# How the first two row blocks are picked out of the tokens in a Trainium2 mixture-of-experts kernel

## What is computed

```python
def moe_ffn(h, router_w, router_bias, w_gate, w_up, w_down):
    scores = jax.nn.sigmoid((t @ router_w).astype(jnp.float32))
    ...
    _, eidx = lax.top_k(jnp.where(emask, sel, -jnp.inf), TOP_K)
    ...
    hg = jnp.einsum('td,edf->tef', t, w_gate)
    hu = jnp.einsum('td,edf->tef', t, w_up)
    act = jax.nn.silu(hg) * hu * comb[:, :, None].astype(t.dtype)
    return jnp.einsum('tef,efd->td', act, w_down).reshape(B, L, D)
```

## Time and profile before

| | |
|---|---|
| runs, median | 1278.73 us |
| the profiled execution | 1281.8 us |
| its span on the core | 1280.1 us |
| PE busy | 1009.5 us (79%) |
| DVE, ACT, POOL busy | 416.9, 229.7, 192.8 us |
| mean granted TensorE clock | 0.907 of 2.4 GHz |
| DMA | 344.59 MB, mean 269 GB/s |

### The profile page before, as it was taken

One profiled execution on the slowest core, in us unless ns is written; L12 is line 12 of the kernel. 1 busy time (PEld: TensorE's weight loads), 2 busy tenths in 40 slices (PEclk: granted clock), 3 DMA queues, 4 the chain that ended last, 5 costly groups with the idle time before them and its releaser, 6 DMA issues.

```text
span 1280.1 us, 24187 instructions
## 1 busy us (share of the span) xinstructions
PE 1009.5 (79%) x9506; PEld 572.9 (45%) x9506; DVE 416.9 (33%) x1139; ACT 229.7 (18%) x459; POOL 192.8 (15%) x382
## 2 busy tenths in 40 slices
PE   0899999789699777796389998988979997775930
PEld 0444447554555444453245554445465553342510
DVE  0220015864612221122553234553542221111207
ACT  0401002431412111111221111110322121110202
POOL 1200000200122221222210000001022221211231
PEclk9999999899689998899689998999959998987975
DMA  9985332967479999999994211444631969999973
GB/s 317 383 277 197 131 139 91 352 246 307 173 278 389 393 402 411 393 396 369 393 378 145 92 66 48 182 197 148 251 160 42 378 236 401 395 398 413 396 274 131
DMA packets 79819, 344.59 MB, mean 269 GB/s; under 512 B 9158, under 2 KB 9609, under 8 KB 67468
## 3 DMA queue, kind: packets, MB, share of 16 engines
q1 hardware_dynamic: 57108, 289.30, 58.4%
q0 software_dynamic: 14608, 43.35, 9.7%
q10 hardware_dynamic: 8040, 11.01, 2.5%
HBM read 320.01 MB, written 23.63 MB: 268 GB/s over the span
## 4 chain that ended last, share of the span: by engine, by line
PE 60%; DMA 20%; DVE 11%; SPq 3%; ACT 3%; issue 2%; POOL 0%; POOLq 0%; DVEq 0%; ACTq 0%; PEldq 0%
PE bank L856 15%; DMA ring<-in_moe_w_up_dram 15%; PE bank L646 11%; PE bank L921 10%; PE bank L772 6%; PE bank L863 6%; DMA ring<-in_ada_w_dram 3%; SPq L1351 3%; PE bank L833 2%; DMA ring<-in_moe_w_down_dram 1%; PE bank L599 1%; PE bank L995 1%; PE bank L1019 1%; ACT arena L1204 1%; DVE arena L1320 1%
## 5 line engine op out<-in xcount | busy, mean ns | idle before, releaser
L856 PE MATMUL bank<-ring,arena 128*32 128x256 f32 x3072 | 193.5, 409 | 50.6 <-DMA ring<-in_moe_w_up_dram 50.6
L856 PEld LDWEIGHTS bank<-ring,arena 128*32 128x32 f32 x3072 | 104.9, 118 | 132.6 <-issue 78.2
L646 PE MATMUL bank<-ring,hT 128*128 128x512 f32 x336 | 144.9, 593 | 1.0 <-ACT hT L1055 1.0
L1318 DVE TENSOR_TENSOR arena<-arena,bank 128x64 f32<-128x64 f32 x136 | 27.4, 202 | 317.0 <-ACT arena L1204 317.0
L921 PE MATMUL bank<-hT,ring 128*128 128x384 f32 x384 | 124.6, 487 | 1.0 <-ACT hT L1055 1.0
L863 PE MATMUL bank<-ring,arena 128*32 128x256 f32 x1536 | 92.8, 382 | 27.3 <-DVE arena L1320 25.4
L599 PE MATMUL bank<-ring,small 128*32 128x256 f32 x768 | 53.8, 443 | 58.7 <-DMA ring<-in_ada_w_dram 58.7
L646 PEld LDWEIGHTS bank<-ring,hT 128*128 128x128 f32 x336 | 63.7, 190 | 80.4 <-issue 79.2
L921 PEld LDWEIGHTS bank<-hT,ring 128*128 128x128 f32 x384 | 72.9, 190 | 52.3 <-ACT hT L1055 1.2
L856 PE MATMUL bank<-arena 128*32 128x256 f32 x1216 | 72.8, 393 | 13.9 <-DMA arena<-in_moe_w_up_dram 13.9
L533 POOL DMA_DIRECT2D arena<-slot_rows x140 | 70.8, 506 | 59.6 <-POOL arena L543 42.8
(11 more groups left out here) (325 smaller groups left out, 1112.6 us busy)
## 6 DMA issues: line engine op xcount, KB each, us to landing
ring<-in_ada_w_dram SPq DMA_DIRECT2D x24, 2048.0 KB, 19.6
ring<-in_moe_w_gate_dram SPq DMA_DIRECT2D x22, 2048.0 KB, 21.9
ring<-in_moe_w_up_dram SPq DMA_DIRECT2D x22, 2048.0 KB, 27.2
ring<-in_moe_w_down_dram SPq DMA_DIRECT2D x22, 2048.0 KB, 30.1
arena<-in_moe_w_gate_dram SPq DMA_DIRECT2D x10, 2048.0 KB, 35.1
arena<-in_moe_w_up_dram SPq DMA_DIRECT2D x10, 2048.0 KB, 40.6
arena<-in_moe_w_down_dram SPq DMA_DIRECT2D x10, 2048.0 KB, 43.9
ring<-in_ev_w_in_dram SPq DMA_DIRECT2D x7, 2048.0 KB, 15.6
```

Of the source, the lines that this page charges most:

```text
L646: last = pe.matmul(bank[3 * (c % 2) + t], hT[:, k, t * P:(t + 1) * P], slot8(n)[:, k, :], start=k == 0, stop=k == KT - 1)
L856: last = pe.matmul(bank[1][q * BLK:(q + 1) * BLK, 0:HALF], slot_inT[:, k, :], both[:, :, k, q * P:(q + 1) * P], start=k == 0, stop=k == KT ...
L1318: dve.tensor_tensor(act_rows[:, two, :], silu_g[:, two, :], up, ALU.mult).then_inc(S["gated"], 1)
```

## The change

It has six parts, in both layers.

1. The picking of block 0 with `h_tok` stationary (L833) goes. Both blocks are picked with 32 columns of `pick` stationary and 512 columns of `h_tok` moving, in the four column groups: 12 matmuls in all.
2. Block 0 now takes the way of the other blocks: ScalarE copies it (64 partitions x 512) to `slot_in`, PE transposes it, DVE copies it to `slot_inT`. ScalarE copies block 1 to `slot_in` after a wait for those transposes.
3. Four matmuls with `ident` stationary and 512 columns of `h_tok` moving go to `bank[3]`, which nothing reads, ahead of the wait for `pick`.
4. PE waits for `table_rdy` and reads the first two limits of its loops before it waits for `pick_rdy`, not after the picking.
5. PE's wait for `trips_rdy` moves to the end of the layer.
6. POOL's wait on its own copies counts one more, since ScalarE now signals twice.

```diff
@@ pool_moe @@
-                    pool.wait_ge(S["row_rdy"], pair * 2 + odd)
+                    pool.wait_ge(S["row_rdy"], pair * 2 + (odd + 1))
@@ pe_moe @@
             pe.wait_ge(htok_act, 6 * (l + 1))
+            for c in range(WARM):
+                pe.matmul(bank[3], ident, h_tok[:, c % NT, 0:512], start=True, stop=True)
+            rows_due = counter(pe, f"rows_due{l}", 1)
+            pe.wait_ge(table_rdy, l + 1)
+            begin, end, after = 0, pe.value_load(table[0:1, 1:2], ...), pe.value_load(table[0:1, 2:3], ...)
             pe.wait_ge(pick_rdy, l + 1)
-            for k in range(KT):
-                h, j = divmod(k, 4)
-                for t in range(NT):
-                    last = pe.matmul(bank[0][:, j * 2 * BLK + h * BLK:j * 2 * BLK + (h + 1) * BLK], h_tok[:, t, k * P:(k + 1) * P],
-                                     pick[:, t, 0:BLK], start=t == 0, stop=t == NT - 1)
-            last.then_inc(S["rowT_mm"], 1)
             for t in range(NT):
                 for q in range(4):
-                    c = (q % 2) * 512 + (q // 2) * HALF
-                    last = pe.matmul(bank[2][q * BLK:(q + 1) * BLK, 0:HALF], pick[:, t, BLK:2 * BLK], h_tok[:, t, c:c + HALF],
-                                     start=t == 0, stop=t == NT - 1)
+                    block, h = divmod(q, 2)
+                    last = pe.matmul(bank[2][q * BLK:(q + 1) * BLK, :], pick[:, t, block * BLK:(block + 1) * BLK],
+                                     h_tok[:, t, h * 512:(h + 1) * 512], start=t == 0, stop=t == NT - 1)
             last.then_inc(pick_mm, 1)
-            pe.wait_ge(table_rdy, l + 1)
-            pe.wait_ge(trips_rdy, l + 1)
...
-            rows_due = counter(pe, f"rows_due{l}", 1)
             pe.sem_inc(S["rowT_mm"], 1)
-            begin, end = 0, pe.value_load(table[0:1, 1:2], ...)
+            rows_to_channels()
             for e in range(NE):
                 n = first + 3 * e
-                after = pe.value_load(table[0:1, e + 2:e + 3], ...) if e + 1 < NE else None
+                if e:
+                    after = pe.value_load(table[0:1, e + 2:e + 3], ...) if e + 1 < NE else None
...
+            pe.wait_ge(trips_rdy, l + 1)
             stores = pe.value_load(trips[0:1, 1:2], ...)
@@ act_moe @@
             act.wait_ge(pick_mm, l + 1)
-            act.activation(slot_in[:, 0:HALF], bank[2][0:2 * BLK, 0:HALF], ACT.Copy)
-            act.activation(slot_in[:, HALF:2 * HALF], bank[2][2 * BLK:4 * BLK, 0:HALF], ACT.Copy).then_inc(S["row_rdy"], 1)
+            act.activation(slot_in, bank[2][0:2 * BLK, :], ACT.Copy).then_inc(S["row_rdy"], 1)
+            act.wait_ge(S["rowT_mm"], 2)
+            act.activation(slot_in, bank[2][2 * BLK:4 * BLK, :], ACT.Copy).then_inc(S["row_rdy"], 1)
```

More of the change, by code:

```diff
@@ L48 @@
 MOE_RING = 9
+WARM = 4
 CHUNK = 4096
@@ L828, in pe_moe @@
             pe.wait_ge(htok_act, 6 * (l + 1))
-            pe.wait_ge(pick_rdy, l + 1)
-            for k in range(KT):
-                h, j = divmod(k, 4)
-                for t in range(NT):
-                    last = pe.matmul(bank[0][:, j * 2 * BLK + h * BLK:j * 2 * BLK + (h + 1) * BLK], h_tok[:, t, k * P:(k + 1) * P],
-                                     pick[:, t, 0:BLK], start=t == 0, stop=t == NT - 1)
-            last.then_inc(S["rowT_mm"], 1)
+            for c in range(WARM):
+                pe.matmul(bank[3], ident, h_tok[:, c % NT, 0:512], start=True, stop=True)
+            rows_due = counter(pe, f"rows_due{l}", 1)
+            pe.wait_ge(table_rdy, l + 1)
+            begin, end, after = 0, pe.value_load(table[0:1, 1:2], min_val=1, max_val=MAX_BLOCKS), pe.value_load(table[0:1, 2:3], min_val=2, max_val=MAX_BLOCKS)
+            pe.wait_ge(pick_rdy, l + 1)
             for t in range(NT):
                 for q in range(4):
-                    c = (q % 2) * 512 + (q // 2) * HALF
-                    last = pe.matmul(bank[2][q * BLK:(q + 1) * BLK, 0:HALF], pick[:, t, BLK:2 * BLK], h_tok[:, t, c:c + HALF],
-                                     start=t == 0, stop=t == NT - 1)
+                    block, h = divmod(q, 2)
+                    last = pe.matmul(bank[2][q * BLK:(q + 1) * BLK, :], pick[:, t, block * BLK:(block + 1) * BLK],
+                                     h_tok[:, t, h * 512:(h + 1) * 512], start=t == 0, stop=t == NT - 1)
             last.then_inc(pick_mm, 1)
-            pe.wait_ge(table_rdy, l + 1)
-            pe.wait_ge(trips_rdy, l + 1)
             def rows_to_channels():
@@ L882, in block_of_expert @@
                 down(s, 3).then_inc(S["down_mm"], 1)
-            rows_due = counter(pe, f"rows_due{l}", 1)
             pe.sem_inc(S["rowT_mm"], 1)
-            begin, end = 0, pe.value_load(table[0:1, 1:2], min_val=1, max_val=MAX_BLOCKS)
+            rows_to_channels()
             for e in range(NE):
                 n = first + 3 * e
-                after = pe.value_load(table[0:1, e + 2:e + 3], min_val=e + 2, max_val=MAX_BLOCKS) if e + 1 < NE else None
+                if e:
+                    after = pe.value_load(table[0:1, e + 2:e + 3], min_val=e + 2, max_val=MAX_BLOCKS) if e + 1 < NE else None
                 for j in range(2):
```

## The result

The changed kernel takes 1271.65 us (median of 11 executions, 1263.81 to 1275.21), the kernel before beside it 1279.39 us. The ratio is 0.9927 with a 95% interval of 0.9907 to 0.9948: faster by 9.3 us (6.7 to 11.9). The two medians are 7.7 us apart, which lies within that interval. One of the eleven executions of the kernel before took 3553.76 us, and the ratio leaves it out. The direction was forecast; the gain is about half of the 17.6 us, and the time lies above the range, which ended at 1268.5.

A forecast was written before the change was run, and what follows sets the result against it. PE at 1.2 GHz bounds `pick` to first gate-and-up, then DMA in layer 0. Stage: 0.6 + 2.65 + 1.7 + 3.5 = 8.45 us for 18.05; after losses 8.3 and 9.3, 17.6 us gained: 1261.1 us, range 1257.5 to 1268.5.

The forecast's parts named there:

- block 0's new way: Between picks and first gate-and-up: ScalarE's copy, transposes, DVE's copy and handovers stand one behind another, 1.7 us a layer.
- four handovers of 0.05: Passing between engines from block 0's picks to its first gate-and-up: 0.05 us each, 0.2 us in all.
- The gate-and-up at 3.5 us: First gate-and-up of each layer's MoE: runs at full clock, 3.54 us in place of 4.94.
- Rival A: Picks to first gate-and-up: clock falls or isn't up, costing 1.4 to 3.1 us a layer, slow picks 2.7 more; chance 0.15.
- Limits first: Ahead of the picks: PE's reading of two loop limits delays their start by 0.6 us a layer, bounds 0 to +1.1.
- Picks: Picking of both blocks in each layer: 24 records at full clock, 2.65 us.
- Rival B: PE's entry into the loop after block 0's transposes is no longer hidden: 1.5 us lost a layer; chance 0.06.
- Block 2's rows: Fetch behind the scatter comes late for PE: some 5 us lost in layer 0, 0.3 in layer 1.
- Layer 0's stream: DMA weight stream in layer 0's MoE: starts 9.6 us earlier less a loss of 1.3, so 8.3 us gained.
- rival C: Layer 0's DMA stream: asking for weights sooner buys little, only 3 to 5 us from that layer; chance 0.11.
- D: Clock stays at 1.2 GHz for long in both layers: 4 us a layer lost, 1286 us; chance 0.03.
- E: Whole kernel: no change, as L833's time would have to be hidden; chance 0.03.

The follow-up runs named there:

- late_scatter: The changed kernel, but POOL starts its six scatters only when DVE has copied block 0: 1275.96 us, ratio 0.9965 to the kernel before.
- profile of after: The profiled execution of the changed kernel, with no further edit, the quickest of its eleven: 1263.81 us.
- again: The changed kernel run and profiled once more with no edit: 1270.33 us, ratio 0.991 to the kernel before.
- cover_more: The changed kernel with unused matmuls added: 768 columns behind the picks, two of 512 behind the first transposes: 1270.39 us, ratio 0.9911.
- warm_only: The kernel before with only the four unused matmuls added ahead of its wait for `pick`: 1275.15 us, ratio 0.995.

## Why the forecast was right in sign and its gain twice the measured one

The step that failed is the sum of block 0's new way, at "four handovers of 0.05". Two of the four, from PE to ScalarE and from PE to DVE, measured 0.76 and 1.46 us in the mean: 2.1 us a layer more than forecast. They were priced from the earlier trace rows, where a PE signal came outside POOL's scatter (360.12 us; the scatter ended at 354.18). The change made the first use of PE signals inside it.

The gate-and-up at 3.5 us was the second term, and it depends on the first. It took 5.50 in the mean, 2.0 more: in five of six stages because the idle PE lost the clock, in the sixth by the break in PE's records at full clock. Where the late signals were gone (late_scatter), so were both: 3.66 in both layers. The picks add 0.4 in the mean, 0.3 of it from the one stage in which the clock fell in them. The limits cost 0.2 less than forecast. 2.1 + 2.0 + 0.4 - 0.2 = 4.3, nearly the whole difference of 13.0 and 8.6.

Rival A, given 0.15, is therefore what came, as a part: its first price, 1.4 to 3.1 a layer, holds the 2.0 of the mean, but it expected the fall from 0.46 busy of 1.7 us. In late_scatter, with that stretch as forecast, the clock held; it fell where PE stood through the late signals as well. The lateness itself stood in none of the rivals.

The other steps:

- *Limits first*, +0.6 (0.74 from `pick`): measured 0.69 and 0.47. The forecast took them as needed there; the runs with the limits behind the picks show that they need cost nothing.
- *Unused matmuls*: hidden, as forecast. They brought full clock to the picks in five of six stages.
- *Picks*, 2.65: 2.78. The 24 loads of weights lie under the matmuls, so the added 0.65 of the rule in the Trainium skill (TensorE: Matmul & The Clock Gate, Part 3) does not appear.
- *ScalarE's copy* 0.59, *transposes* 0.43, *DVE's copy* 0.42: forecast 0.60, 0.46, 0.42.
- *Rival B*, the loop's entry: PE starts 0.06 after DVE's copy ends (352.00 to 352.06), so the entry itself costs nothing. But something of B's kind came a few records later: the break in layer 1 (945.05 to 945.85) makes the gate-and-up 0.64 longer than 3.66. In all runs together seven first gate-and-ups ran at full clock and began before POOL had ended its scatter; each took 4.30 to 5.29 us, with such a break, and went on in full 1.1 to 1.3 us after the scatter's end. Of those at full clock that began after its end, or before its start (late_scatter), each took 3.66. So this time goes with the scatter too. That the code of the loop comes late to PE would fit; no run tests it.
- *Block 2's rows*: layer 0 transposes them at 367.35 after 4.00 us of idle (forecast 367.8 and 5), layer 1 doesn't wait.
- *Layer 0's stream* (rival C): SP's gate matrices go out 8.0 us earlier than before the first two times, 2.9 to 3.5 the next four (387.64 against 390.55 the first of them), and again 8.3 and 8.0 at 451.08 and 510.87. PE, late with block 2, asks later for a while, but the DMA stream has enough ahead of it, as forecast. The loss was 0.2, 1.2 and 3.4 us, forecast 1.3. Layer 0 as a whole, from `pick` to its last gate-and-up, gave 5.5, 1.7 and 2.1 us in the three profiles. In the mean that is the 3 to 5 us that C named, but most of it was missing in the stage already and not in the stream: C's number without its mechanism.
- *D*, slower, and *E*, no change, did not come.
- Both of the prediction's own signs of being wrong came: the clock wasn't held in five of six stages, and layer 0 didn't keep its 8 us.

What would have shown it beforehand: the old L833 and L839 were queued on PE for the whole scatter, so no engine waited for a PE signal while POOL issued it. The trace of before had no row for this handover, and 0.05 should have had an upper bound.

Shown: the lateness goes where the scatter goes, stays with a sixteenth of the bytes, and is not brought forward by queued work. Only argued: that the making of the descriptors holds PE's signals, rather than something else that six such instructions do; by what path is open. Open too: what breaks PE's records until the scatter has ended, and whether the limits behind the picks win in the program. A scatter that another engine issues, or that is split so that its instructions stand apart, was not tried.

## What to carry to other kernels

When a change breaks one long queue on an engine into short steps that hand over to others, price each handover from a row in which the same neighbours are at work, above all GpSimd with indirect DMAs; where there is no such row, give it an upper bound. Dense work ahead of a wait lifts the clock for what follows, but the next idle stretch decides whether the work behind it keeps it. When an engine's own long work gets short, look again at what it hid: here the reading of the limits and the loop's first records. Measure such a stage in several profiles: the same kernel's took 10.4 to 15.3 us.

## What the runs showed of the hardware

- In the semaphore events of the traces, of 445 PE records that signal none in the kernel before came over 0.12 us after its modelled end. In the changed kernel's three profiles it is four each, the picks and the first transposes of both layers, 0.3 to 1.7 us late. For DVE and ScalarE the list has no late event, but it lacks the events of several of their copies in this stretch; there the engine that waited started 0.14 us (PE after ScalarE) and 0.06 us (PE after DVE) after the copy's end.
- In the profile of after these four come 0.27 to 0.63 us after the start of one of POOL's scatter instructions, which follow each other every 1.27 us. In `again` the second of layer 0 came 1.0 us after the end of the last one. More work queued on PE moved the second to 3.1 us, and in late_scatter it was 5.7, past the whole scatter.
- PE works on while its signals are late: it went from the picks into the next matmul without a gap (cover_more), and from a gate-and-up into the transposes (late_scatter). It isn't free of the scatter, though: eight stretches of records that were under way when it ended (seven gate-and-ups, and the picks of block 1 in layer 1 of warm_only) have a break that lasts until 1.1 to 1.3 us after its end, with no wait for a semaphore.
- In warm_only the clock fell during the old picks (32 moving columns, 128 stationary ones) though PE was never idle, 3.5 us after they began in layer 0 and 5.1 in layer 1. In the kernel before it stays at 1.2 GHz for their whole 10.42 us.
